# A two-layer transformer block on one core: convolution tiles first in the first linear stage of both layers

## What is computed

```python
for i in range(DEPTH):
    u = h @ w_in[i]                                  # 272 tokens, 1024 -> 3840 columns
    q, k, v = u[..., :512], u[..., 512:640], u[..., 640:768]
    y_attn = sliding_window_attention(q, k, v, sinks[i], rel_bias) @ w_attn_proj[i]
    y_conv = conformer_conv(u[..., 768:1792], ...) @ w_conv_proj[i]
    mix = (sigmoid(u[..., 1792:2816]) * y_attn + sigmoid(u[..., 2816:]) * y_conv) @ w_out[i]
    h = layer_norm(ALPHA * h + mix, ...)
    h = layer_norm(ALPHA * h + ffn(h), ...)          # dense in layer 0, 8 experts in layer 1

def conformer_conv(u, dw, db, g, b):
    val, gate = split(u)
    h = val * sigmoid(gate)                          # 512 channels
    h = depthwise_conv(h, dw, taps=31) + db          # causal, 31 taps
    return silu(layer_norm(h, g, b))
```

## Time and profile before

| | us |
|---|---|
| median of 3 runs (lowest to highest) | 3707.21 (3706.18 to 3708.64) |
| the profiled execution, its time | 3708.28 |
| the profiled execution, its span | 3706.5 |
| PE busy in the span | 3417.7 (92%) |
| DVE busy | 1905.1 (51%) |
| ACT busy | 1565.2 (42%) |
| POOL busy | 311.4 (8%) |

### The profile page before, as it was taken

The page is one execution under the profiler, slowest core; times in us unless marked ns, Lnnn a source line. Parts: engine busy times, 40 slices in busy tenths (PEclk is TensorE's granted clock), DMA queues, the critical chain, the costliest instruction groups (busy, mean ns, idle before and its releaser), DMA issues.

```text
span 3706.5 us, 56512 instructions
## 1 busy us (share of the span) xinstructions
PE 3417.7 (92%) x20954; PEld 3003.4 (81%) x20954; DVE 1905.1 (51%) x2972; ACT 1565.2 (42%) x2486; POOL 311.4 (8%) x380
## 2 busy tenths in 40 slices
PE   7679998679999999998999999989999899987898
PEld 6669998569999999998888777668887788864798
DVE  3955558557666666665333333643333433346554
ACT  4344443345655555655322234533222422244444
POOL 1700007400000000001000011210000100010000
PEclk8769999589999999999999999989999999998999
DMA  6303543326666666764222221112222122220253
GB/s 218 112 23 141 179 164 126 86 94 238 251 246 228 229 239 245 255 242 155 88 103 85 88 80 62 40 57 81 108 80 107 65 78 110 77 91 12 81 187 109
DMA packets 83870, 487.57 MB, mean 132 GB/s; under 512 B 10945, under 2 KB 18721, under 8 KB 39818
## 3 DMA queue, kind: packets, MB, share of 16 engines
q1 hardware_dynamic: 77456, 469.86, 35.4%
q0 software_dynamic: 4224, 12.83, 1.2%
q10 hardware_dynamic: 1978, 1.75, 0.1%
HBM read 483.03 MB, written 10.74 MB: 133 GB/s over the span
## 4 chain that ended last, share of the span: by engine, by line
PE 85%; DVE 8%; ACT 3%; issue 1%; DMA 1%; POOL 0%; ACTq 0%; SPq 0%; DVEq 0%; POOLq 0%
PE PS L763 24%; PE PS L764 24%; PE PS L765 24%; PE PS L800 4%; PE PS L890 3%; DVE CONV L1504 3%; PE PS L869 2%; DVE WL L1319 2%; PE PS L844 1%; PE PS L879 1%; PE PS L848 1%; DVE RSTD L1336 1%; DMA bias_rows<-bias_row 1%; ACT H L1055 0%; PE PS L909 0%
## 5 line engine op out<-in xcount | busy, mean ns | idle before, releaser
L1319 DVE TENSOR_TENSOR WL<-RAW,WH 128x1024 fp32r<-128x1024 f32 (+1 forms) x972 | 1092.5, 1129 | 911.4 <-ACT WH L1034 885.9
L763 PE MATMUL PS<-UH,WH 128*128 128x256 f32 (+2 forms) x4192 | 1360.9, 325 | 133.9 <-DVE UL L1352 64.9
L1034 ACT ACTIVATE WH<-RAW 128x1024 fp32r<-128x1024 f32 (+1 forms) x972 | 948.7, 978 | 1098.4 <-PE PS L765 1057.8
L764 PE MATMUL PS<-UL,WH 128*128 128x256 f32 (+2 forms) x4192 | 1359.7, 324 | 0.0
L765 PE MATMUL PS<-UH,WL 128*128 128x256 f32 (+2 forms) x4192 | 1356.6, 324 | 0.0
L763 PEld LDWEIGHTS PS<-UH,WH 128*128 128x128 f32 x4192 | 810.7, 193 | 209.6 <-issue 140.1
L765 PEld LDWEIGHTS PS<-UH,WL 128*128 128x128 f32 x4192 | 810.6, 193 | 58.2
L764 PEld LDWEIGHTS PS<-UL,WH 128*128 128x128 f32 x4192 | 809.1, 193 | 59.5
L763 PE MATMUL PS<-HIDH,WH 128*128 128x256 f32 (+2 forms) x1584 | 502.2, 317 | 0.0
L765 PE MATMUL PS<-HIDH,WL 128*128 128x256 f32 (+2 forms) x1584 | 502.2, 317 | 0.0
L764 PE MATMUL PS<-HIDL,WH 128*128 128x256 f32 (+2 forms) x1584 | 502.1, 317 | 0.0
(11 more groups left out here) (157 smaller groups left out, 2609.7 us busy)
## 6 DMA issues: line engine op xcount, KB each, us to landing
RAW<-in_w_gu SPq DMA_DIRECT2D x198, 1024.0 KB, 4.8
RAW<-in_w_dn SPq DMA_DIRECT2D x144, 704.0 KB, 4.1
RAW<-in_w_mod SPq DMA_DIRECT2D x72, 1024.0 KB, 5.0
RAW<-in_w_in SPq DMA_DIRECT2D x30, 1024.0 KB, 5.0
RAW<-in_w_na SPq DMA_DIRECT2D x12, 1024.0 KB, 4.8
RAW<-in_w_proj SPq DMA_DIRECT2D x8, 1024.0 KB, 4.9
RAW<-in_w_out SPq DMA_DIRECT2D x8, 1024.0 KB, 4.8
RAW<-in_w_o SPq DMA_DIRECT2D x8, 1024.0 KB, 4.8
```

What stands on the lines that cost most here:

```text
L763: pe.matmul(ps, wh, mh, start=opens and x == 0, stop=False)
L764: pe.matmul(ps, wh, ml, start=False, stop=False)
L1034: act.activation(WH[slot][:, 0:hi - lo], RAW[:, s % RAW_SLOTS, lo:hi], ACT.Copy).then_inc(s_hi, 1)
L1319: dve.tensor_tensor(WL[slot][:, 0:hi - lo], RAW[:, s % RAW_SLOTS, lo:hi], WH[slot][:, 0:hi - lo].bitcast(F32), ALU.subtract).then_inc(s_lo, 1)
```

## The change

The order of the 15 tiles becomes: steps 0 to 3 the convolution's input, steps 4 to 6 queries, keys and values, steps 7 to 14 the gates as before. DVE's wait for the zeros of `HPAD` now stands ahead of step 0. The convolution starts at step 4 and does three taps in each of eleven steps (the last does one). POOL's convolution starts after the evacuation of step 3 instead of step 6, and its wait for the queries moves behind its convolution. The five DMAs that fill `B1` go from POOL's queue to SP's, behind the load of step 14; POOL keeps the write and the broadcast in DRAM, with the wait for the broadcast, ahead of the zeros.

```diff
+WIN_TILES = [3, 4, 5, 6, 0, 1, 2] + list(range(7, 15))
+CONV_FROM, CONV_TAPS = 4, 3
...
-        add(f"win{i}", 1, "aaa" + "dddd" + "a" * 8)
+        add(f"win{i}", 1, "dddd" + "aaa" + "a" * 8)
...
+            def bias_tiles(layer):
+                if layer == 0:
+                    sp.wait_ge(s_browd, 32)
+                sp.wait_ge(s_pc, ph[f"win{layer}"].p0)
+                for q, (q0, nq) in enumerate(((0, NMETA), (NMETA, P), (NMETA + P, P))):
...
+                        sp.dma_start(B1[q][0:nq, :, k0:k0 + n], src).then_inc(s_b1, 16)
...
-                straight(f"win{i}", ins["w_in"][i])
+                for s, t in enumerate(WIN_TILES):
+                    load(ph[f"win{i}"], 0, s, ins["w_in"][i][t])
+                bias_tiles(i)
...
-            def bias_tiles(layer):
+            def bias_row_copies(layer):
                 if layer == 0:
                     pool.wait_ge(s_brow, 4)
...
                     pool.dma_start(bias_rows, bias_row.to_broadcast([8, P, 2 * BW])).then_inc(s_browd, 16)
                     pool.wait_ge(s_browd, 32)
-                for q, (q0, nq) in enumerate(((0, NMETA), (NMETA, P), (NMETA + P, P))):
...
-                        pool.dma_start(B1[q][0:nq, :, k0:k0 + n], src).then_inc(s_b1, 16)
...
-                pool.wait_ge(s_evd, ph[f"win{layer}"].evacs("d", 0, 7))
+                pool.wait_ge(s_evd, ph[f"win{layer}"].evacs("d", 0, 4))
...
-                bias_tiles(i)
+                bias_row_copies(i)
                 pool.memset(HPAD[:, :, 0:TAPS - 1], 0.0).then_inc(s_ms, 1)
...
-                pool.wait_ge(s_eva, ph[f"win{i}"].evacs("a", 0, 3))
-                pool.wait_ge(s_zero, i + 1)
...
                 pool.wait_ge(s_pcv, (i + 1) * POOL_STEPS)
+                pool.wait_ge(s_eva, ph[f"win{i}"].evacs("a", 0, 7))
+                pool.wait_ge(s_zero, i + 1)
...
-                for s in range(3):
-                    ahead(p, 0, s)
                 dve.wait_ge(s_ms, 4 + i)
-                for s in range(3, 7):
+                for s in range(4):
                     ahead(p, 0, s, (0,))
                     multiplied(dve, p, 0, s)
...
                     ahead(p, 0, s, (1,))
-                dve.wait_ge(s_evd, p.evacs("d", 0, 7))
-                for s in range(7, 15):
+                dve.wait_ge(s_evd, p.evacs("d", 0, 4))
+                for s in range(CONV_FROM, 15):
                     ahead(p, 0, s)
-                    conv(i, c0, n, 4 * (s - 7), min(4 * (s - 6), TAPS))
+                    conv(i, c0, n, CONV_TAPS * (s - CONV_FROM), min(CONV_TAPS * (s - CONV_FROM + 1), TAPS))
```

More of the change, by code:

```diff
@@ L571, in experts @@
                 iterate(sp, p, body)
+            def bias_tiles(layer):
[3 more added lines that the diff above has]
+                for q, (q0, nq) in enumerate(((0, NMETA), (NMETA, P), (NMETA + P, P))):
+                    nk = q0 + nq
+                    pieces = [(0, 0, NMETA)] + ([(1, NMETA, nk - NMETA)] if q else [])
+                    for v, k0, n in pieces:
+                        src = bass.AP(tensor=bias_rows.tensor, offset=v * BW + L1 - q0 + k0,
+                                      ap=[[2 * BW - 1, nq], [2 * P * BW, 8], [1, n]])
+                        sp.dma_start(B1[q][0:nq, :, k0:k0 + n], src).then_inc(s_b1, 16)
             for i in range(DEPTH):
@@ L636, in bias_tiles @@
                     pool.wait_ge(s_browd, 32)
-                for q, (q0, nq) in enumerate(((0, NMETA), (NMETA, P), (NMETA + P, P))):
-                    nk = q0 + nq
-                    pieces = [(0, 0, NMETA)] + ([(1, NMETA, nk - NMETA)] if q else [])
-                    for v, k0, n in pieces:
-                        src = bass.AP(tensor=bias_rows.tensor, offset=v * BW + L1 - q0 + k0,
-                                      ap=[[2 * BW - 1, nq], [2 * P * BW, 8], [1, n]])
-                        pool.dma_start(B1[q][0:nq, :, k0:k0 + n], src).then_inc(s_b1, 16)
             def stage_queries(a, it, half, src, c0, n):
@@ L1207, in _ @@
                 p = ph[f"win{i}"]
-                for s in range(3):
-                    copy_step(p, 0, s, (Q1[:, 2 * s, :], Q1[:, 2 * s + 1, :]), L1, SCALE if s < 2 else 1.0)
-                for s in range(3, 7):
+                for s in range(4):
                     ahead(p, 0, s, (0,))
                     multiplied(act, p, 0, s)
-                    if s >= 5:
+                    if s >= 2:
                         act.wait_ge(s_evd, p.evacs("d", 0, s - 1))
@@ L1216, in _ @@
                     ahead(p, 0, s, (1,))
+                for s in range(3):
+                    copy_step(p, 0, 4 + s, (Q1[:, 2 * s, :], Q1[:, 2 * s + 1, :]), L1, SCALE if s < 2 else 1.0)
                 for s in range(7, 15):
@@ L1518, in _ @@
                 p = ph[f"win{i}"]
-                for s in range(3):
-                    ahead(p, 0, s)
                 dve.wait_ge(s_ms, 4 + i)
-                for s in range(3, 7):
+                for s in range(4):
                     ahead(p, 0, s, (0,))
                     multiplied(dve, p, 0, s)
-                    dve.wait_ge(s_sil, SIL_BASE[f"win{i}"] + s - 2)
-                    dve.tensor_tensor(HPAD[:, s - 3, TAPS - 1:TAPS - 1 + L1], PS[2 * (s % BANK_SETS)][:, 0:L1],
+                    dve.wait_ge(s_sil, SIL_BASE[f"win{i}"] + s + 1)
+                    dve.tensor_tensor(HPAD[:, s, TAPS - 1:TAPS - 1 + L1], PS[2 * (s % BANK_SETS)][:, 0:L1],
                                       TMP[:, s % 2, 0:L1], ALU.mult).then_inc(s_evd, 1)
                     ahead(p, 0, s, (1,))
-                dve.wait_ge(s_evd, p.evacs("d", 0, 7))
-                for s in range(7, 15):
+                dve.wait_ge(s_evd, p.evacs("d", 0, 4))
+                for s in range(CONV_FROM, 15):
                     ahead(p, 0, s)
-                    conv(i, c0, n, 4 * (s - 7), min(4 * (s - 6), TAPS))
+                    conv(i, c0, n, CONV_TAPS * (s - CONV_FROM), min(CONV_TAPS * (s - CONV_FROM + 1), TAPS))
                 dve.wait_ge(s_b1, 16 * 5 * (i + 1))
```

## The result

The changed kernel takes 3692.7 us (median of 7 runs, 3688.23 to 3699.35), the kernel before in the same comparison 3710.5 (7 runs, 3706.18 to 3721.44). The profiled execution took 3690.57 us with a span of 3688.8; before it was 3708.28 and 3706.5. The spans differ by 17.7 us. The forecast was 3691.6, with a range of 3685.5 to 3699.5.

What follows compares the result with a forecast made beforehand. DVE was taken as the bound in both layers' first linear stages, in layer 0 after waiting for POOL's zeros. Gains of 11.3 (layer 1) and 4.3 (layer 0) make 15.6 us less, 3691.6 us, range 3685.5 to 3699.5.

Steps and rivals of the forecast that it cites:

- Layer 1, convolution 18.15 earlier: Layer 1: four steps instead of seven at PE's 6.05 us stand ahead of the convolution, so it starts 18.15 us earlier.
- six more pieces at 1.14: Layer 1: six more weight pieces fall inside DVE's convolution, at 1.14 us each, 6.8 us lost.
- about one addition of POOL's per pair: Convolution: DVE loses about one POOL addition, 0.77 us, per pair of POOL's instructions, whatever else DVE does in between.
- a few tenths lost: Last three convolution steps, POOL done: DVE's step of 6.1 us is just PE's pace, a few tenths lost.
- zeros 11.1 earlier at 60.3: Layer 0: no DMA issues ahead and a broadcast running alone bring the zeros at 60.3 instead of 71.35, 11.1 us earlier.
- The rule of the Trainium skill that was weighed: One core's HBM limit, some 358 GB/s: by it loads didn't slow layer 0's broadcast, zeros only 4.1 us earlier.
- Layer 0, gain 4.3: Layer 0: zeros 11.1 us earlier, less 6.8 for six extra weight pieces, gain 4.3 us.
- The bias tiles on SP at nothing: Both layers: bias tiles issued on SP some 45 us before the attention needs them stay hidden and cost nothing.
- a wait for `WH` in the convolution's steps: Sign named beforehand: DVE waiting for `WH` in the convolution's steps would make the prediction wrong.
- The rival of the clock: Convolution's eleven steps: PE's clock stays at 1.2 GHz, a step costs 12.1 us, time about 3785 us; chance 0.04.
- The sum: Whole kernel: 11.3 us from layer 1 plus 4.3 from layer 0, 15.6 us less, giving 3691.6 against the median.
- the other price: A weight piece beside POOL's work costs DVE 2.56 / 2 = 1.28 us; in both layers 1.8 us more, 3693.4.

Runs made afterwards that it cites:

- run 1: The changed kernel with the five bias-tile DMAs back on POOL's queue, behind the broadcast and ahead of the zeros: 3698.72 us, ratio 0.9971.
- run 2: The kernel before with only the five bias-tile DMAs moved to SP, order of the tiles unchanged: 3707.17 us, ratio 0.9992.
- run 5: The changed kernel with the new order of the tiles but four taps a step instead of three: 3705.74 us, ratio 0.9982.
- run 8: The changed kernel with zeros written ahead of the broadcast, the last tap moved to step 12, and without POOL's last wait for the broadcast: 3672.07 us, ratio 0.9884.
- run 6: The changed kernel with the last tap given to earlier steps, so step 12 does four taps and step 14 none: 3689.94 us, ratio 0.9931.
- run 9: The changed kernel with POOL's additions of the convolution on one column, its multiplications whole: 3662.71 us, one execution.

## Why the prediction was right, point by point

**Layer 1, convolution 18.15 earlier:** from the last inputs of the stage (539.41 before, 532.43 after) to the convolution's start it takes 48.8 before and 30.6 after, 18.2 less. Right.

**Layer 1, six more pieces at 1.14:** they cost 72.40 to 80.69, less the 1.36 of idle time, 6.93 us, or 1.16 a piece. Right. The price at which the pieces lie outside POOL's account was the one to take, and its reason, a fixed number of POOL's instructions that each take their share, fits; but the share is not "about one addition of POOL's per pair": it is 0.50 of the addition and 0.18 of the product, and the sum only happens to be near an addition's 0.77.

**Layer 1, "a few tenths lost" in the last three steps:** this is the step that failed. It compared DVE's step with PE's in general, and did not ask into which buffers the next stage's first two pieces go. The loss, which the sum put at nothing, was 1.36 us, in both layers, and it is the whole difference between the gain of 11.3 that was forecast for layer 1 and the 9.9 measured.

**Layer 0, zeros 11.1 earlier at 60.3:** they were done at 58.66, 12.7 earlier than at 71.35. The cause was right (runs 1 and 2), and the rate too, 0.195 MB/us against 0.193. Of the 1.6 us beyond the forecast 0.98 is that the broadcast was issued earlier (38.86 against 39.84): 0.4 is the start of the program, and 0.6 that POOL waited less for the bias row ahead of it, 2.07 us instead of 2.66. The remaining 0.6 I can't assign. The rule of the Trainium skill that was weighed ("DMA: Bandwidth & Descriptors", section "Bandwidth") would, as it was used, have left the broadcast as slow as it was, since two queues together moved less than its limit for one core; 27.0 us beside the loads in run 2 and 19.6 without them speak against using it so. The prediction counted the broadcast's bytes once, but it reads DRAM and writes it. Counted twice, as an estimate, the traffic was (3.07 + 2 x 1.75) / 16 = 0.41 MB/us beside the loads and 2 x 0.195 = 0.39 alone, both above that limit. So the limit can't be used here either way, and what holds back the two queues no run shows.

**Layer 0, gain 4.3:** measured 4.4, by luck, from two errors that cancel. From the end of the norm the convolution starts 12.8 earlier where 11.1 was said, and 8.4 instead of 6.8 is lost behind it, 1.36 of it the wait for `WH`. Some 0.5 of the earlier start lies behind the zeros: when PE set in again, it ran at half clock for 4.3 us (60.42 to 64.71), before for 5.4 (73.12 to 78.54). What the prediction did not say is how little the order does here: by runs 1 and 2 its faster broadcast only pays for its six pieces, and the 4.4 us are the move's.

**The bias tiles on SP at nothing:** right. Issued at 118 and 596, they landed within 5.0 to 6.1 us, and no one waited for `B1`. Two of the rows of the DMA issues, which answer to the earlier trace rows:

```profile
B<-bias_rows SPq DMA_DIRECT2D x2, 1024.0 KB, 5.8
...
B<-bias_rows SPq DMA_DIRECT2D x2, 8.0 KB, 5.0
```

The text called a wait for `WH` in the convolution's steps a thing that would make the prediction wrong; it was there, and cost 2.7 us in all. So the time was right with a part of the mechanism wrong.

**The rival of the clock:** refuted. DVE, not PE, set the pace. The two stretches of layer 0's convolution with the lowest clock up to 140:

```profile
110.00:115.00 5.00, 5.00 (x33) 5.00 (x32) 5.00 (x8) 1.06 (x1) 4.75 (x7) 0.75 0.59 210
...
125.00:130.00 5.00, 4.51 (x24) 4.54 (x25) 5.00 (x8) 0.00 (x0) 4.83 (x4) 0.66 1.06 340
```

DVE is busy for 5.00 of 5.00 us in each. The nine stretches from 95 to 140 have clocks between 0.66 and 1.00, mean 0.92, above the 0.71 from which it would have decided. The waits of PE for the pieces were 0.3 to 2.7 us. After each of the three of 2.7 us in layer 0 the clock fell soon after work set in again, and PE ran at half clock for 3.2 to 3.4 us before it came back. So the form of the rival was there in every second step, and DVE's longer step hid it. From one such wait's end to the next (108.32 to 125.49) 17.2 us pass, as long as DVE's two steps.

**The sum:** 15.6 forecast, 14.3 found as the change's own. That the total came within 1.1 us of 3691.6 is luck. The other 3.4 us of the 17.7 are start, norm and end, of which no step had spoken; and by the medians the gain is 17.8, from 3710.5, while the forecast took 15.6 from 3707.2, the median of the first three runs. Layer 1's gain was right for the reasons given, but for the one step; layer 0's came out by cancelling errors.

**Small slips in the working.** 3.8 + 2.3 + 3.8 + 2.3 + 1.3 is 13.5, not 13.4. 2.35 / 2 is 1.18; the 1.14 is half of the 2.27 us to the next instruction's start, and the other price, taken the same way, is 1.24 and not 1.28. The times given for layer 1 (570, 649.3) leave out layer 0's gain, which comes ahead of them: with it the attention would be at 645.0, and it was at 643.71.

**What stays open:** why the broadcast, alone, moves 0.195 MB/us and not more; what sets the clock in the norm (the lower or the higher level in kernels that differ only ahead of it); why the untouched rest takes 3044 to 3056 us, a spread that is larger than the 4 to 5 us by which the medians of runs 5 and 8 differ from what their traces show. The buffers' numbers were not changed in a run; the reading rests on the code, on run 6 and on run 5.

## What to carry to other kernels

When the work of one engine is spread to cover another's, ask of the last pieces into which buffer they go and who still reads it: at the seam of two stages a ring that starts anew can shorten the lookahead. A short write that others wait for belongs ahead of a long transfer in its engine's program: the 0.2 us of zeros, written first, were worth 12.8 us in layer 0 of the kernel before, nearly as much as the whole change, and 18.2 on top of it. And steps moved to a place behind a wait bring nothing there, if they are the work that filled the wait. When a change has two parts, run each alone: here one part made layer 0's gain and the other layer 1's.

## What the runs showed of the hardware

DVE's multiply-add of 128x272 takes 0.42 us alone, 0.48 beside POOL's products, 0.53 beside products and copies, 0.63 beside additions and 0.66 beside both. The Trainium skill, in "SBUF — State Buffer", section "Who interferes with whom", calls the port that the two share an exclusive lock. The trace agrees for DVE's pieces: an instruction of POOL that meets two of them takes 2.98 us instead of 1.15, some 1.8 of the pieces' 2.35 us. For the multiply-adds it does not look like that: a product of POOL lasts 1.0 to 1.15 us in the changed kernel and 1.55 to 1.95 in run 9, and takes 0.18 us from DVE there.

The broadcast of 3200 KB took 19.5 to 19.9 us alone and 26.9 to 30.9 beside loads of 1 MB each. The issues of the five `B1` transfers took 4.1 us of POOL's queue and 5.2 to 5.7 of SP's. From SP's queue they landed in 5.0 to 6.1 us in the changed kernel, whatever their size, from 8 to 1024 KB; from POOL's, in the kernel before, in 2.1 to 9.1, by size.
